# Dots of half the tokens by TensorE for all experts, gathered with a copied value row

## What is computed

```python
def peer(h, w_q, keys, u_tab, v_tab):
    tok = h.reshape(-1, PEER_BLOCK, D)                      # 4 blocks of 128 tokens
    def block(xb):
        q = (xb @ w_q).reshape(T, PEER_HEADS, 2, PEER_HALF)
        s = jnp.einsum('thpd,hpnd->thpn', q, keys)
        sv, si = lax.top_k(s, PEER_TOPK)                    # 16 of 128, two sides
        ...                                                 # top 16 of 256 sums: eid, cv
        g = jax.nn.softmax(cv, axis=-1)
        u = jnp.take(u_tab, eid, axis=0)                    # 16384 experts x 1024
        act = jax.nn.gelu(jnp.einsum('thkd,td->thk', u, xb))
        return jnp.einsum('thk,thkd->td', g * act, jnp.take(v_tab, eid, axis=0))
```

## Time and profile before

| | us |
|---|---|
| median of 3 runs | 2097.53 (2096.0 to 2109.05) |
| profiled execution, first to last instruction | 2089.7 |
| start of gather 0, 80, 256, 384 | 582.8, 859.2, 1408.0, 1738.3 |
| start of the last gather (511) | 2067.2 |

### The profile page before, as it was taken

The page is one execution under the profiler, slowest core; times in us unless marked ns, Lnnn a source line. Parts: engine busy times, 40 slices in busy tenths (PEclk is TensorE's granted clock), DMA queues, the critical chain, the costliest instruction groups (busy, mean ns, idle before and its releaser), DMA issues.

```text
span 2089.7 us, 15934 instructions
## 1 busy us (share of the span) xinstructions
PE 1518.5 (73%) x4648; PEld 876.7 (42%) x4648; DVE 1491.0 (71%) x2906; ACT 497.1 (24%) x1412; POOL 878.6 (42%) x658
## 2 busy tenths in 40 slices
PE   7899999889667778887865778655555555556564
PEld 3465787668545555564531445311111111111111
DVE  2545368763276667878598856688898898898876
ACT  2201120111222233223233322222222223222222
POOL 2478404220033333343345434345554555455553
PEclk9899899999879899999987899877777767676677
DMA  8233221124278999999999999799999999999997
GB/s 348 101 139 138 89 79 61 62 77 144 81 308 353 362 351 345 410 392 387 421 393 361 386 378 347 282 413 387 413 412 422 403 409 387 409 417 409 406 418 294
DMA packets 90604, 647.28 MB, mean 310 GB/s; under 512 B 10413, under 2 KB 10773, under 8 KB 12565
## 3 DMA queue, kind: packets, MB, share of 16 engines
q0 software_dynamic: 76448, 555.78, 66.7%
q1 hardware_dynamic: 13376, 90.25, 11.2%
q10 hardware_dynamic: 693, 0.23, 0.0%
HBM read 644.12 MB, written 2.10 MB: 309 GB/s over the span
## 4 chain that ended last, share of the span: by engine, by line
PE 42%; DMA 21%; DVE 19%; issue 8%; ACT 7%; POOL 2%; SPq 0%; DVEq 0%; ACTq 0%; POOLq 0%
DMA arena<-in_peer_uv,arena 21%; PE bank L917 13%; PE bank L671 11%; DVE arena L1642 6%; PE bank L887 6%; PE bank L856 4%; DVE arena L1657 3%; PE bank L707 3%; POOL arena L613 2%; ACT smalls L1138 2%; ACT arena L1133 1%; ACT arena L1128 1%; PE bank L906 1%; PE bank L697 1%; PE bank L800 1%
## 5 line engine op out<-in xcount | busy, mean ns | idle before, releaser
L613 POOL DMA_INDIRECT arena<-in_peer_uv,arena x512 | 688.8, 1345 | 901.4 <-DVE arena L1657 571.1
L917 PE MATMUL bank<-arena,smalls 128*128 128x512 f32 x1024 | 700.9, 822 | 477.6 <-ACT smalls L1138 470.7
L1642 DVE CUSTOM_DVE_ANT_0 arena<-arena 128x1024 f32<-128x1024 f32 x512 | 615.1, 1221 | 87.5 <-DMA arena<-in_peer_uv,arena 86.1
L917 PEld LDWEIGHTS bank<-arena,smalls 128*128 128x128 f32 x1024 | 225.7, 241 | 887.8 <-ACT smalls L1138 675.2
L1657 DVE SCALAR_TENSOR_TENSOR arena<-arena 128x1024 f32<-128x1024 f32 x252 | 322.0, 1278 | 204.8 <-ACT arena L1133 204.8
L671 PE MATMUL bank<-arena 128*128 128x256 f32 (+1 forms) x1216 | 336.1, 433 | 3.6 <-ACT arena L962 3.4
L671 PEld LDWEIGHTS bank<-arena 128*128 128x128 f32 x1216 | 235.9, 195 | 104.6 <-issue 76.0
L1128 ACT ACTIVATE arena<-arena 128x2 f32<-128x2 f32 x256 | 51.9, 203 | 778.0 <-DVE arena L1642 776.3
L887 PE MATMUL bank<-arena 128*128 128x256 f32 x512 | 125.4, 402 | 0.7 <-issue 0.7
L1133 ACT ACTIVATE arena<-arena 128x1 f32<-128x1 f32 x512 | 122.9, 287 | 8.5
L887 PEld LDWEIGHTS bank<-arena 128*128 128x128 f32 x512 | 106.2, 208 | 35.9 <-issue 21.5
(11 more groups left out here) (241 smaller groups left out, 1311.5 us busy)
## 6 DMA issues: line engine op xcount, KB each, us to landing
arena<-in_w_in SPq DMA_DIRECT2D x40, 1024.0 KB, 6.2
arena<-in_w_ada POOLq DMA_DIRECT2D x16, 1024.0 KB, 5.1
arena<-in_w_out SPq DMA_DIRECT2D x16, 1024.0 KB, 6.8
arena<-in_peer_w_q SPq DMA_DIRECT2D x16, 1024.0 KB, 9.9
arena<-in_w_ada SPq DMA_DIRECT2D x8, 1024.0 KB, 9.2
arena<-in_peer_uv,arena POOLq DMA_INDIRECT x512
arena<-in_x SPq DMA_DIRECT2D x4, 512.0 KB, 11.3
out<-arena SPq DMA_DIRECT2D x4, 512.0 KB
```

Of the source, the lines that this page charges most:

```text
L613: nc.gpsimd.indirect_dma_start(gslot[n % NGS], None, uv_tab[0], bass.IndirectOffsetOnAxis(eid[t % 2][:, k:k + 1], 0)).then_inc(s_gsl[n % N ...
L917: last = mm(acc[h][:, :], diag[:, j % NDG], row_v(n)[:, h * 512:(h + 1) * 512], start=(i == 0), stop=(i == BT - 1))
L1642: V.tensor_tensor_reduce(row_u(n), row_u(n), h2[t], 1.0, 0.0, ALU.mult, ALU.add, dots[:, k:k + 1]).then_inc(s_dot, 1)
```

## The change

Two ways to the dots now. For tiles 0 and 1 gathers stay as they are. For tiles 2 and 3 PE computes, for all 16384 experts, the dot of u with each of the 256 tokens: u comes as 64 loads of 1 MB (in_peer_u_cols, 256 experts each) through SP's ring, expert_scores(c) makes 16 matmuls 128x256 of each, ACT puts them through gelu into a staging buffer sst of two, and SP stores them to a table in DRAM, values_scores, of 1280 words a row: scores of tile 2, value row, scores of tile 3. The value rows are copied there from DRAM to DRAM by 64 copies of 1 MB that SP issues behind the loads from xbc_0 on (4 each for 8 loads, then 2 each for 16). A gather for tile 2 or 3 brings 1152 words (4608 bytes): the 128 scores and the value row. DVE then picks each token's own score by multiplying with the identity and the gate (for the odd row that is already the diagonal), in pick_dense; ACT has no part in these pairs.

To have the tokens of tiles 2 and 3 early, the side steps of the second half go two to a pair, pairs 0 to 39. From there, at a pace of 7.0 / 6.5 pairs for a score step and 3.0 / 6.5 for a query step: 28 scores (pairs 40 to 70), 12 query steps (70 to 75), 20 scores (75 to 97), 12 query steps (100 to 105), 16 scores (105 to 122). In tiles 0 and 1 PE takes every fourth value row instead of every second, and DVE the rest. POOL waits at gather 256 for all copies and stores.

```diff
...
     NPK = LT * NE
+    NROW = NPK // LT * NA
+    NEXP = u_cols.shape[0] * WCOL
+    NS = u_cols.shape[0]
+    VSW = D + 2 * P
+    VCOL, SCOL = P, (0, P + D)
+    GW_ROW, VLO, SLO = D + P, (P, 0), (0, D)
...
-    side = [s for u in units[2:NUA] for s in unit_steps(u)]
-    side += late
-    UB = 88
-    assert len(side) < UB
-    side += [[] for _ in range(UB - len(side))]
-    side[UB - 2].append(("h2T", NA))
-    side[UB - 1].append(("h2T", NA + 1))
-    side += [s for u in units[NUA:] for s in unit_steps(u)]
+    first = [s for u in units[2:NUA] for s in unit_steps(u)] + late
+    first += [[("h2T", NA)], [("h2T", NA + 1)]]
+    side = [[] for _ in range(NBT)]
+    for n, items in enumerate(first):
+        side[n // 2] += items
+    S_A, S_B = 28, 48
+    half_u = (len(units) - NUA) // 2
+    block = [[s for u in units[NUA + i * half_u:NUA + (i + 1) * half_u] for s in unit_steps(u)] for i in range(2)]
+    score = lambda a, b: [[("S", c)] for c in range(a, b)]
+    pace = lambda items: 7.0 if items[0][0] == "S" else 3.0
+    at_j = len(first) / 2
+    for earliest, part in ((0, score(0, S_A)), (0, block[0]), (0, score(S_A, S_B)), (100, block[1]),
+                           (0, score(S_B, NS))):
+        at_j = max(at_j, earliest)
+        for items in part:
+            side[int(at_j)] += items
+            at_j += pace(items) / 6.5
+    assert at_j < NA * BT
...
         BSEQ.append(("pk", j))
-        if j < len(side):
-            BSEQ += side[j]
+        BSEQ += side[j]
...
         arena = sb("arena", [P, 196 * KB])
+        vs = nc.dram_tensor("values_scores", [NEXP, VSW], F32).ap()
+        vs_rows = vs.rearrange("e (a t) -> (e a) t", t=P)
...
         sBt = at(176, 2, 512)
+        sst = at(176, 2, 2, NA, P)
...
         def row_v(n):
-            return gslot[n % NGS][:, D:2 * D]
+            lo = D if n < NROW else VLO[n // NE - NA]
+            return gslot[n % NGS][:, lo:lo + D]
+        def row_s(n):
+            lo = SLO[n // NE - NA]
+            return gslot[n % NGS][:, lo:lo + P]
+        def by_pe(n):
+            return n % 2 == 1 if n >= NROW else n % 4 == 3
+        pe_rows = list(itertools.accumulate(int(by_pe(n)) for n in range(NPK)))
+        def dve_rows(n):
+            return n + 1 - pe_rows[n]
...
-        def query_loads(half):
-            wq_0[half] = len(loads)
-            for n in range(2 * QB):
+        q_load, s_load = {}, {}
+        def query_loads(half, q4s):
+            for n in range(2 * q4s[0], 2 * q4s[-1] + 2):
                 last = [u for u in units if u[1] == n // 2 and u[0] in halves[half]][-1]
+                q_load[half, n] = len(loads)
                 add_load(w_q, n, ("q", *last))
+        def score_loads(a, b):
+            for c in range(a, b):
+                s_load[c] = len(loads)
+                add_load(u_cols, c, ("S", c))
         mixer_loads(0)
-        query_loads(0)
+        query_loads(0, range(QB))
         mixer_loads(1)
-        query_loads(1)
+        late_x = len(loads)
+        score_loads(0, S_A)
+        query_loads(1, range(QB // 2))
+        score_loads(S_A, S_B)
+        query_loads(1, range(QB // 2, QB))
+        score_loads(S_B, NS)
+        NCOPY = 64
+        CROW = NEXP // NCOPY
+        copies, copied = {}, 0
+        for n in range(xbc_0, proj_load["gc", 0, 0] + 3 * NX // 2):
+            more = 4 if n < z_0[0] else 2
+            copies[n] = range(copied, min(copied + more, NCOPY))
+            copied += len(copies[n])
+        assert copied == NCOPY
...
         def _(sp):
+            def store_scores(c):
+                await_read(sp, ("S", c))
+                for m, col in enumerate(SCOL):
+                    dst = vs[c * WCOL:(c + 1) * WCOL, col:col + P].rearrange("(j e) t -> e j t", e=P)
+                    sp.dma_start(dst, sst[:, c % 2, :, m]).then_inc(s_sst[c % 2], 16)
+            stored = 0
             sp.dma_start(rowA, rows_a).then_inc(s_rows, 16)
             for n, (w, j) in enumerate(loads):
-                if n == wq_0[1]:
+                if n == late_x:
...
                 sp.dma_start(wring[:, n % WRING].rearrange("p k n -> p (k n)"), w[j]).then_inc(s_w[n % WRING], 16)
+                for i in copies.get(n, ()):
+                    rows_ = slice(i * CROW, (i + 1) * CROW)
+                    sp.dma_start(vs[rows_, VCOL:VCOL + D], uv_tab[0][rows_, D:2 * D]).then_inc(s_vcopy, 16)
+                while stored < NS and s_load[stored] < n - WRING:
+                    store_scores(stored)
+                    stored += 1
+            for c in range(stored, NS):
+                store_scores(c)
...
                     pool.wait_ge(s_eid, h + 1 if h < 2 else h // 2 + 2)
+                if n == NROW:
+                    pool.wait_ge(s_vcopy, 16 * NCOPY)
+                    for i in range(2):
+                        pool.wait_ge(s_sst[i], 16 * NS)
                 if n >= NGS:
-                    if n % 2:
-                        pool.wait_ge(s_peused, (n - NGS) // 2 + 1)
+                    if by_pe(n - NGS):
+                        pool.wait_ge(s_peused, pe_rows[n - NGS])
                     else:
-                        pool.wait_ge(s_vadd, (n - NGS) // 2 + 1)
-                nc.gpsimd.indirect_dma_start(
-                    gslot[n % NGS], None, uv_tab[0], bass.IndirectOffsetOnAxis(eid[t % 2][:, k:k + 1], 0)
-                ).then_inc(s_gsl[n % NGS], 16)
+                        pool.wait_ge(s_vadd, dve_rows(n - NGS))
+                which = bass.IndirectOffsetOnAxis(eid[t % 2][:, k:k + 1], 0)
+                if n < NROW:
+                    nc.gpsimd.indirect_dma_start(gslot[n % NGS], None, uv_tab[0], which).then_inc(s_gsl[n % NGS], 16)
+                else:
+                    nc.gpsimd.indirect_dma_start(gslot[n % NGS][:, 0:GW_ROW], None, vs_rows, which
+                                                 ).then_inc(s_gsl[n % NGS], 16)
...
+            def expert_scores(c):
+                ps = claim(("S", c))
+                if c == 0:
+                    await_read(pe, ("h2T", LT - 1, 1))
+                w = weights(s_load[c])
+                for j in range(2):
+                    dst = ps[:, j * NA * P:(j + 1) * NA * P].rearrange("p (m t) -> p m t", m=NA)
+                    for k in range(KD):
+                        last = mm(dst, w[:, k, j * P:(j + 1) * P], h2T[:, :, k, :], start=(k == 0), stop=(k == KD - 1))
+                filled(last, ("S", c))
             def add_row(j):
-                t, i, n = j // BT, j % BT, 2 * j + 1
-                acc = [claim(("vs", t, h)) if i == 0 else bank_of(("vs", t, h)) for h in range(2)]
-                pe.wait_ge(s_diag, j + 1)
-                landed(pe, n)
-                for h in range(2):
-                    last = mm(acc[h][:, :], diag[:, j % NDG], row_v(n)[:, h * 512:(h + 1) * 512],
-                              start=(i == 0), stop=(i == BT - 1))
-                    if i == BT - 1 and h == 0:
-                        filled(last, ("vs", t, 0))
-                if i < BT - 1:
-                    last.then_inc(s_peused, 1)
-                else:
-                    filled(last, ("vs", t, 1))
-                    await_filled(pe, ("vs", t, 1))
-                    nc.tensor.sem_inc(s_peused, 1)
+                for n in (2 * j, 2 * j + 1):
+                    if not by_pe(n):
+                        continue
+                    t, q = n // NE, pe_rows[n] - 1
+                    begin = q == (pe_rows[t * NE - 1] if t else 0)
+                    end = pe_rows[n] == pe_rows[(t + 1) * NE - 1]
+                    acc = [claim(("vs", t, h)) if begin else bank_of(("vs", t, h)) for h in range(2)]
+                    if n < NROW:
+                        pe.wait_ge(s_diag, q + 1)
+                    else:
+                        pe.wait_ge(s_diagd, q + 1 - pe_rows[NROW - 1])
+                    landed(pe, n)
+                    for h in range(2):
+                        last = mm(acc[h][:, :], diag[:, q % NDG], row_v(n)[:, h * 512:(h + 1) * 512],
+                                  start=begin, stop=end)
+                        if end and h == 0:
+                            filled(last, ("vs", t, 0))
+                    if end:
+                        filled(last, ("vs", t, 1))
+                        await_filled(pe, ("vs", t, 1))
+                        nc.tensor.sem_inc(s_peused, 1)
+                    else:
+                        last.then_inc(s_peused, 1)
             parts = {"h2T": queries_T, "q": query_half, "qT": query_T, "s": scores, "pk": add_row,
-                     "z": lambda hq, i: z_part(hq, 1, i), "proj": lambda n: proj(n, 1), "yT": y_transpose,
+                     "S": expert_scores, "z": lambda hq, i: z_part(hq, 1, i), "proj": lambda n: proj(n, 1), "yT": y_transpose,
...
+                if 2 * j >= NROW:
+                    return
...
                       scale=gelu[:, k + i:k + i + 1]).then_inc(s_wexp, 1)
-                act.wait_ge(s_wexp, 2 * j + 2)
-                if j >= NDG:
```

(75 more changed lines are left out.)

12 lines of the change are left out of this document (6 added, 6 removed).

## The result

The changed kernel takes 2277.4 us (median, 2276.3 to 2283.3) against 2096.8 for the kernel before, measured beside it: a ratio of 1.0857, with an interval of 1.0822 to 1.0892. It is 180 us slower. The forecast was 2109 with a range up to 2190, so the size was wrong and the time lies above the range. "Slower" had the largest chance, 0.48, but 0.32 of it came from rivals B and C; the forecast by itself gave 0.15 to it.

A forecast was written before the change was run, and what follows sets the result against it. It took DMA to bound the kernel from the first gather on, with POOL next in tiles 2 and 3. 582.8 + 12 + 1070 + 436 = 2101 us of span, plus 7.8, gave 2109; range 2015 to 2190.

The forecast's parts named there:

- rival B: Tiles 0 and 1: ACT waits for an earlier store of scores before reusing a staging buffer; +75 us, 2184; chance 0.20.
- rival C: Before the gathers: DRAM-to-DRAM copies run at half rate, 329 us, 60 over the free time; 2157 us; chance 0.14.
- The first stage: Before gather 0: the 64 copies mostly fit into free DMA time, adding 12 us to 582.8.
- Gathers 0 to 255: Tiles 0 and 1: added transfers and PE work make the stage 1070 us instead of 825, bounds 960 and 1160.
- 300 + 463 + 127: PE's work in tiles 0 and 1: 300 us of other work, 463 of score groups, 127 of value rows.
- 64 x 1.7 = 109: Tiles 0 and 1: PE idles 1.7 us before each of 64 value rows, waiting for ACT's chain; 109 us.
- the factor of 1.07: Tiles 0 and 1: measured 825 us over the same reckoning's 771 before the change; raises PE's sum 999 to 1069.
- Gathers 256 to 511 and the tail: Tiles 2 and 3: shorter gathers take 436 us in place of 681.7, bounds 398 and 486.
- 1.60 us a gather: Tiles 2 and 3: POOL sets the pace, 0.94 instruction + 0.30 gap + 0.36 hold behind DVE.
- Rival A: Transfer rate rules everywhere, once POOL needs under 1.45 us a gather; stages 997 and 398, total 1986 us; chance 0.22.
- The bound of 1.67 us: Tiles 2 and 3: upper DMA time per gather, 589.8 KB at 354 GB/s, read from loads at 5 to 9 us.
- the 1.45 us of the forecast: Tiles 2 and 3: DMA time per shortened gather, by bytes at 408 GB/s.

The follow-up runs named there:

- the swap: The changed kernel, two staging buffers kept, with SP issuing each store of scores ahead of the next 1 MB load instead of behind it: 2195.6 us.
- the mended kernel: The changed kernel with four staging buffers, scores copied out after the next pair's diagonal, ten slots in tiles 2 and 3, every eighth value row on PE: 2010.8 us.

## Why the prediction was wrong

**The first stage (12 us, measured 2.5).** Right in kind. The copies went near the rate of loads: the share of 0.63 over 585 us in place of 0.33 over 583 is 176 us more of all 16 engines for 67.1 MB, an estimate of 381 GB/s, against the 164 us by the rate of loads and the 329 of rival C, which is out. The Trainium skill's price for copies between HBM tensors ("DMA: Bandwidth & Descriptors", "Latency and other measured facts", 207 to 214 GB/s in each direction) is not what rows of 4 KB did here. The page measured rows of 16 KB, at row pitches of 512 KB and of 4 MB plus 4 KB. Traffic and issues of the changed kernel from 27 to 450 us, where four copies follow each load at first:

```profile
DMA  9999999999999994976703999009670299225730
GB/s 418 396 371 372 411 395 377 380 359 383 401 342 367 318 363 131 371 258 261 291 0 102 346 342 370 34 0 325 272 272 27 99 339 350 108 72 225 279 120 0
...
values_scores<-in_peer_uv SPq DMA_DIRECT2D x64, 1024.0 KB, 12.9
```

**Gathers 0 to 255 (1070 us, measured 1203; bounds 960 and 1160).** This is the step that failed. The work on PE was nearly right: 300 + 463 + 127 = 890 forecast, 931 measured. The rows took 178 us busy in place of 127, part of them at the lower clock level (a mean of 854 ns an instruction, where 1.98 us a row is 495), the scores 457 and the rest 295. What failed is the term "64 x 1.7 = 109" for PE's wait for ACT's diagonal. The group in the changed kernel, from 585 to 1788 us:

```profile
L996 PE MATMUL bank<-arena 128*128 128x256 f32 x2048 | 457.4, 384 | 1.1 <-issue 0.8 <-PE bank L1014 0.3
L1014 PE MATMUL bank<-arena,smalls 128*128 128x512 f32 x249 | 178.1, 854 | 244.0 <-ACT smalls L1239 244.0
```

244 us idle ahead of the rows, 3.8 each: 135 more than forecast. (The stage missed by 133. The 41 us more of work are made up by the factor of 1.07 for all else, 70 us, of which 28 were used.) The experiments part the 244, taken in the order in which they were made:

- 66 went when ACT no longer waited for stores (four buffers, 177.5 left). This is rival B.
- 63 more went when ACT made the diagonal ahead of the copy (late eviction, 114.2 left). The forecast knew that the copy stands ahead of the gelu and gave it no price beyond the 1.7.
- 114.2, about the forecast of 109, remain. So the 1.7 fits a wait in which nothing else holds ACT; many single waits of the changed kernel are 1.73 us, as that of 1081.16.

The 1.7 had been read off one query, where ACT's copy had nothing to wait for but PE. Rival B had the mechanism written down, at 0.20, with its price (75 us) and its point (a landing of 12 us against 9.1 between two groups). The landing was 10.5 us in the case shown, and the time against it was not 9.1 but 7.0, since PE does the groups two by two: the mean pace was used where the second of a couple sets the wait. Measured by taking it away, rival B is worth 91 us of the stage and 98 of the time, 82 by the swap alone.

Rival B alone would have given 2184, and the time was 2277. The stage without the store's hold is 1112, 42 over the 1070; the late eviction brings it to 1043. Another 50 us of the gap are the next point.

**Gathers 256 to 511 and the tail (436 us, measured 486; bound 486).** The value 1.60 us a gather was worked out from POOL's hold behind DVE's instructions (0.36). In the change the hold was 0.10 (1.04 us an instruction against 0.94) and POOL's pace 1.34, so by POOL alone the stage should have been shorter than forecast. It was longer, because of a term that was not in the sum at all: the round of a slot. Ten slots in place of six gave 73 us, so that is what set 1.83 us a gather. With ten slots POOL's instruction was 1.18 us, a hold of 0.24, and a gather took 1.55. That suggests that the small hold of the change came in part from POOL and DVE standing idle. Rival A asked for POOL under 1.45, which it was, and still the transfers did not rule: its condition was not sufficient.

The bound of 1.67 us for a gather by DMA rested on a misread stretch. From 5 to 9 us the profile counts 392 packets, 233 of them under 2 KB and only 5 between 2 and 8 KB, so it was no stretch of 4 KB rows. The gathers of 4608 bytes themselves reached 375 to 389 GB/s, 1.55 us.

The joins of the sum: -9.5 us in the first stage, +133 in the second, +50 in the third, 173.5 of span; 2101 + 173.5 = 2274.5, as measured.

**Rival A** lost as stated, but it is where the mended kernel goes: 358 us for the first 40 pairs and 685 for the rest is 1043 against its 997, and 395 with ten slots against its 370.

## What to carry to other kernels

When a step that stores its result is put on an engine that others wait for, count the buffers by the store's landing time, not by the compute between two: issue to landing was 10 us with 1 MB loads in the same queue, and with 7 us of work in each, two buffers were too few and four took the wait away. A falling DMA share with more bytes is the sign to look for a wait. When a transfer is made shorter, ask whether its slots still cover a slot's round: six did for 8 KB rows and did not for 4.6 KB. And waits for stores of 234 us cost 98 us in one version, while 275 us of them cost nothing in another where the transfers are full (share 0.99), so a wait's worth is found by taking it away in the version that it is in.

## What the runs showed that I had not expected

Copies inside DRAM in rows of 4 KB went near the rate of loads, beside the loads (359 to 418 GB/s for both in the first eleven slices), and the loads of w_ada on the other queue took 9.0 us to land in place of 5.1 without making the first stage longer by more than 2.5 us.

Gathers of 4608-byte rows reached 375 to 389 GB/s at a share of 0.98 to 1.00, under the 408 of 8192-byte rows, so the 1.45 us of the forecast should be 1.55.

POOL's indirect DMA instruction fell from a mean of 1.38 us to 1.04 when DVE's dots had gone and its additions of 1.27 us stayed. With ten slots it was 1.18, with DVE busy 85% as in the kernel before, so it seems that the dots are one part of the difference and DVE's idle time another.

The mended kernel is faster than both: 2010.8 us against 2098.4 for the kernel before, measured beside it. What is left open is the price of the dense second half of the mixer: pairs 0 to 39 take 326 us at the best against 276 before, and nothing was tried on them but the share of rows.
